# Forgetting attention: decay added by VectorE with the row maximum; second top-16 step over 112 sums instead of 256

## The reference

```python
# forgetting attention, 8 heads of 128
s = jnp.einsum('bqhd,bkhd->bhqk', qb, k) * scale
s = s + (F[q] - F[k])            # F = cumsum(log sigmoid(forget logit))
p = jax.nn.softmax(jnp.where(q_pos >= k_pos, s, NEG_INF))
# PEER routing, 8 heads, 128 + 128 keys
v1, i1 = lax.top_k(s1, 16);  v2, i2 = lax.top_k(s2, 16)
cand = v1[..., :, None] + v2[..., None, :]          # 16 x 16 = 256 sums
sc, sel = lax.top_k(cand.reshape(..., 256), 16)
expert = i1[sel // 16] * 128 + i2[sel % 16];  gate = softmax(sc)
```

## Time and profile before

| | us |
|---|---|
| median of 3 runs (4210.09 to 4221.3) | 4219.01 |
| the profiled execution | 4219.77 |
| its span, first to last instruction | 4218.0 |
| PE busy (matmul) | 3439.9 |
| DVE busy | 2838.2 |
| POOL busy | 1438.0 |
| ACT busy | 381.5 |
| granted TensorE clock, mean | 0.90 |
| DMA, mean over the span | 335 GB/s |

### The profile page before, as it was taken

How to read it: one execution, slowest core, us unless ns; L and a number is a source line. 1 busy time by engine, 2 the same in 40 slices (tenths; PEclk the granted TensorE clock), 3 DMA queues, 4 the chain that set the end, 5 groups by cost and what they waited for, 6 DMA issues and landing times.

```text
span 4218.0 us, 39029 instructions
## 1 busy us (share of the span) xinstructions
PE 3439.9 (82%) x14249; PEld 2539.4 (60%) x14249; DVE 2838.2 (67%) x3456; ACT 381.5 (9%) x954; POOL 1438.0 (34%) x1094
## 2 busy tenths in 40 slices
PE   7899999999999989999988789999939999930000
PEld 5466678888845546567766567777727777720000
DVE  5354442237777875775677888887885555579998
ACT  0311110000211111010000011001000000010000
POOL 0000000000025443442343442324352665577764
PEclk9999999999999998989999899999969999965555
DMA  8577555567359998999999996889989999989997
GB/s 326 209 273 291 207 198 207 200 235 277 147 235 397 375 375 353 389 374 381 415 409 411 412 374 270 316 333 383 417 334 377 419 409 409 413 312 408 410 396 319
DMA packets 251315, 1412.71 MB, mean 335 GB/s; under 512 B 35313, under 2 KB 83457, under 8 KB 86145
## 3 DMA queue, kind: packets, MB, share of 16 engines
q0 software_dynamic: 124704, 841.18, 49.5%
q1 hardware_dynamic: 68832, 501.25, 30.4%
q10 hardware_dynamic: 57632, 68.41, 4.6%
HBM read 1359.60 MB, written 51.16 MB: 334 GB/s over the span
## 4 chain that ended last, share of the span: by engine, by line
PE 42%; DMA 22%; DVE 20%; POOL 7%; issue 4%; DVEq 2%; ACT 1%; PEld 0%; ACTq 0%; PEldq 0%; SPq 0%; POOLq 0%
PE pq L434 42%; DMA first<-peer_v,experts 10%; DMA first<-peer_u,experts 9%; DVE pq L1727 5%; POOL first L1885 4%; DVE late L1727 3%; DVE first L1717 3%; DMA ring<-wstream 3%; POOL got L1903 2%; DVE ring L1266 1%; DVE late L1264 1%; DVE arena L1500 1%; DVE arena L1507 1%; POOL ring L1885 1%; DVE arena L1501 1%
## 5 line engine op out<-in xcount | busy, mean ns | idle before, releaser
L434 PE MATMUL pq<-h_last,ring 128*128 128x288 f32 (+2 forms) x6688 | 1670.7, 412 | 52.0 <-DVEq L1469 34.5
L434 PEld LDWEIGHTS pq<-h_last,ring 128*128 128x128 f32 (+2 forms) x6688 | 1272.9, 191 | 440.7 <-DVEq L1469 38.1
L1885 POOL DMA_INDIRECT first<-peer_u,experts x256 | 394.3, 1540 | 1734.8 <-DVEq L1562 1213.1
L1885 POOL DMA_INDIRECT first<-peer_v,experts x464 | 640.1, 1380 | 872.4 <-DVEq L1728 788.6
L1727 DVE SCALAR_TENSOR_TENSOR late<-first,wts,late 128x2048 f32<-128x2048 f32 x254 | 597.3, 2351 | 200.7 <-DMA first<-peer_v,experts 189.1
L1717 DVE CUSTOM_DVE_ANT_0 first<-first,late 128x2048 f32<-128x2048 f32 x256 | 582.4, 2291 | 213.1 <-DMA first<-peer_u,experts 204.8
L434 PE MATMUL pq<-first,ring 128*128 128x256 f32 (+2 forms) x3104 | 686.8, 383 | 13.1 <-DMA ring<-wstream 6.6
L434 PEld LDWEIGHTS pq<-first,ring 128*128 128x128 f32 (+2 forms) x3104 | 577.7, 187 | 116.1 <-issue 10.5
L1727 DVE SCALAR_TENSOR_TENSOR pq<-first,wts,pq 128x2048 f32<-128x2048 f32 x142 | 334.4, 2355 | 113.2 <-DMA first<-peer_v,experts 103.9
L1903 POOL DMA_INDIRECT got<-dots_dram,at_dot x288 | 322.8, 1121 | 105.6 <-issue 105.0
L434 PE MATMUL pq<-arena,ring 128*128 128x256 f32 (+2 forms) x1216 | 298.4, 406 | 43.0 <-issue 30.4
(11 more groups left out here) (197 smaller groups left out, 2061.7 us busy)
## 6 DMA issues: line engine op xcount, KB each, us to landing
ring<-wstream SPq DMA_DIRECT2D x478, 1024.0 KB
dots_dram<-wts ACTq DMA_DIRECT2D x8, 2304.0 KB, 8.4
dots_dram<-stage ACTq DMA_DIRECT2D x128, 144.0 KB
first<-peer_v,experts POOLq DMA_INDIRECT x464
got<-dots_dram,at_dot POOLq DMA_INDIRECT x288
first<-peer_u,experts POOLq DMA_INDIRECT x256
out<-arena ACTq DMA_DIRECT2D x6, 512.0 KB, 7.5
o_last<-x_t ACTq DMA_DIRECT2D x5, 576.0 KB, 17.0
```

What stands on the lines that cost most here:

```text
L434: return nc.tensor.matmul(out, lhsT, rhs, start=start, stop=stop)
L1885: g.indirect_dma_start(out=slots[slot], out_offset=None, in_=peer_u if kind == "u" else peer_v, in_offset=bass.IndirectOffsetOnAxis(ap=exp ...
```

## The change

The decay leaves the matmuls. `frow` keeps only -F; one DRAM tensor `forget` holds it, and `load_forget` (one DMA on ACT's queue) broadcasts one head's row to all 128 partitions: 256 elements in group 0, 672 in group 1. DVE waits for it ahead of `row_max`, which adds it to the scores in PSUM and takes the maximum in one instruction, `tensor_tensor_reduce`. F[q] is left out: it is the same for a whole row, so the softmax does not see it. The stores and loads of the rows of ones go.

The second `top16` looks at 112 sums: those of the 4 best of the first list with all 16 of the second, and those of the 12 others with the 4 best of the second. A pair (a, b) of ranks counted from 0 is beaten by (a+1)(b+1) - 1 others, so no other pair can be among the 16 best. The position has to be decoded in another way, and the picking of the two halves is no longer in pairs but one after the other. Some renamings are left out below.

```diff
-        aug_q = [area("misc", WG[1], 2), area("latT", WG[1], 2, NH * PAST)]
-        aug_k = [area("misc", NKEY, 2, WG[1]), area("latT", NKEY, 2, NH * PAST + WG[1])]
+        forget = [area("misc", NKEY), area("latT", NKEY, P, NH * PAST)]
...
+        NF = 4 * TOPK + 4 * (TOPK - 4)
...
+                self.cand, self.cand_rest = self.pairs[:, :, 0:NF], pairs_rest[:, :, 0:NF]
+                self.cand_wide = self.pairs[:, :, 0:4 * TOPK].rearrange("p t (a b) -> p t a b", a=4)
+                self.cand_deep = self.pairs[:, :, 4 * TOPK:NF].rearrange("p t (a b) -> p t a b", b=4)
...
             def scores_fox(g, h):
-                if g == 0:
-                    pe.wait_ge(aug_in[0], 32 * (h + 1))
-                else:
-                    pe.wait_ge(aug_in[h % 2], 32 * (h // 2 + 1) + (32 * NH if h % 2 == 0 else 0))
...
-                    for c0, c1, keys_of, at in parts:
-                        mm(ps[:, c0:c1], qn[:, q], keys_of, True, False)
-                        last = mm(ps[:, c0:c1], aq[:, q], ak[:, at:at + c1 - c0], False, True)
+                    for c0, c1, keys_of in parts:
+                        last = mm(ps[:, c0:c1], qn[:, q], keys_of)
...
-            act.dma_start(aug_q_dram[:, 1, :], aug_ones[:, 0:T]).then_inc(aug_st, 16)
-            act.dma_start(aug_k_dram[:, 0, :], aug_ones).then_inc(aug_st, 16)
...
-                act.dma_start(aug_q_dram[:, 0, CG[g]:CG[g + 1]], frow[:, 0, 0:w]).then_inc(aug_st, 16)
                 kw_ = w + (PAST if g else 0)
-                act.dma_start(aug_k_dram[:, 1, CG[g]:CG[g] + kw_], frow[:, 1, 0:kw_]).then_inc(aug_st, 16)
+                act.dma_start(forget_dram[:, CG[g]:CG[g] + kw_], frow[:, 0:kw_]).then_inc(forget_st, 16)
...
-            def load_aug(g, i):
+            def load_forget(g, i):
                 b = i % 2 if g else 0
-                act.dma_start(aug_q[b][:, 0:WG[g]], aug_q_dram[i, :, CG[g]:CG[g + 1]]).then_inc(aug_in[b], 16)
                 kw_ = NKEY if g else WG[0]
-                act.dma_start(aug_k[b][:, 0:kw_], aug_k_dram[i, :, 0:kw_]).then_inc(aug_in[b], 16)
+                act.dma_start(forget[b][:, 0:kw_], forget_dram[i:i + 1, 0:kw_].to_broadcast([P, kw_])).then_inc(forget_in[b], 16)
...
             def evict_fox(g, i):
                 if i > 0:
                     act.wait_ge(kt_ps, NH * g + i)
+                    act.wait_ge(mx_ok, head(g, i, True))
                     if g == 0:
                         act.wait_ge(kA_st, 16 * i)
-                        load_aug(0, i)
+                        load_forget(0, i)
...
-                    v.reduce_max(stat[0:m, 2, t:t + 1], pb[b][0:m, c:c + SC_W[g][i]], AX.X)
+                    d = pb[b][0:m, c:c + w]
+                    if less is None:
+                        v.reduce_max(stat[0:m, 2, t:t + 1], d, AX.X)
+                    else:
+                        k0 = 0 if t < QT else TP
+                        v.tensor_tensor_reduce(out=d, in0=d, in1=less[0:m, k0:k0 + w], scale=1.0, scalar=-3.0e38,
+                                               op0=ALU.add, op1=ALU.max, accum_out=stat[0:m, 2, t:t + 1])
...
-                    row_max(g, head(g, i, True), cn["mask_fox"], 1.0)
+                    if g == 0:
+                        dve.wait_ge(forget_in[0], 16 * (i + 1))
+                    else:
+                        dve.wait_ge(forget_in[i % 2], 16 * (i // 2 + 1) + (16 * NH if i % 2 == 0 else 0))
+                    row_max(g, head(g, i, True), cn["mask_fox"], 1.0, forget[i % 2 if g else 0])
...
-                    va = r.top_v[:, :, 0, :].rearrange("p t (k o) -> p t k o", o=1).to_broadcast(full)
-                    vb = r.top_v[:, :, 1, :].rearrange("p t (o k) -> p t o k", o=1).to_broadcast(full)
-                    v.tensor_tensor(r.hots[0], va, vb, ALU.add)
+                    for dst, a0, a1, nb in ((r.cand_wide, 0, 4, TOPK), (r.cand_deep, 4, TOPK, 4)):
+                        part = [P, nt, a1 - a0, nb]
+                        va = r.top_v[:, :, 0, a0:a1].rearrange("p t (k o) -> p t k o", o=1).to_broadcast(part)
+                        vb = r.top_v[:, :, 1, 0:nb].rearrange("p t (o k) -> p t o k", o=1).to_broadcast(part)
+                        v.tensor_tensor(dst, va, vb, ALU.add)
...
                     v.tensor_scalar(r.sel_a, r.sel, 4, None, ALU.logical_shift_right)
-                    v.tensor_scalar(r.sel_b, r.sel, 15, None, ALU.bitwise_and)
-                    dve.drain()
-                    v.tensor_copy(r.sel_f[:, 0], r.sel_a)
-                    v.tensor_copy(r.sel_f[:, 1], r.sel_b)
+                    v.tensor_scalar(r.sel_b, r.sel, 2, None, ALU.logical_shift_right)
+                    dve.drain()
+                    v.scalar_tensor_tensor(r.sel_f[:, 0], r.sel_b, -12.0, r.sel_a, ALU.add, ALU.max)
                     dve.drain()
...
+                    v.tensor_scalar(r.ex_f, r.sel_f[:, 0], 4.0, 48.0, ALU.mult, ALU.add)
+                    chosen(0)
+                    dve.drain()
+                    v.scalar_tensor_tensor(r.ex_f, r.sel_f[:, 0], 16.0, r.ex_f, ALU.mult, ALU.min)
+                    dve.drain()
+                    v.tensor_tensor(r.sel_f[:, 1], r.sel, r.ex_f, ALU.subtract)
+                    numbered(0)
+                    dve.drain()
+                    v.reduce_sum(r.sel_f[:, 0], r.hots[0], AX.X)
+                    chosen(1)
+                    dve.drain()
+                    numbered(1)
+                    dve.drain()
+                    v.reduce_sum(r.sel_f[:, 1], r.hots[1], AX.X)
```

More of the change, by code:

```diff
@@ L164, in build @@
     dots_dram = nc.dram_tensor("dots_dram", (NK * NK, TD), F32).ap()
-    aug_k_dram = nc.dram_tensor("aug_k", (NH, 2, NKEY), F32).ap()
+    forget_dram = nc.dram_tensor("forget", (NH, NKEY), F32).ap()
     with ExitStack() as ctx:
@@ L207, in build @@
         F_W = WG[1] + PAST
-        frow = area("probT", 2 * F_W, NH).rearrange("p (r t) -> p r t", r=2)
+        frow = area("probT", F_W, NH)
         merged = [arena[:, 0:KC * w].rearrange("p (k t) -> p k t", k=KC) for w in WG]
@@ L244, in __init__ @@
                 self.s_rest = route(nl * NK, "p (t s n) -> p t s n", t=nt, s=2)
-                self.cand = route(nt * NC, "p (t n) -> p t n", t=nt)
+                self.pairs = route(nt * NC, "p (t n) -> p t n", t=nt)
                 self.top_v = route(nl * TOPK, "p (t s k) -> p t s k", t=nt, s=2)
@@ L254, in __init__ @@
                 self.sel_b = route(nt * TOPK, "p (t k) -> p t k", U32, t=nt)
-                self.cand_rest = self.s_rest.rearrange("p t s n -> p t (s n)")
-                self.hots = [x.rearrange("p t (k j) -> p t k j", k=TOPK) for x in (self.cand, self.cand_rest)]
+                pairs_rest = self.s_rest.rearrange("p t s n -> p t (s n)")
+                self.hots = [x.rearrange("p t (k j) -> p t k j", k=TOPK) for x in (self.pairs, pairs_rest)]
+                self.cand, self.cand_rest = self.pairs[:, :, 0:NF], pairs_rest[:, :, 0:NF]
+                self.cand_wide = self.pairs[:, :, 0:4 * TOPK].rearrange("p t (a b) -> p t a b", a=4)
+                self.cand_deep = self.pairs[:, :, 4 * TOPK:NF].rearrange("p t (a b) -> p t a b", b=4)
         routing = [Routing(len(GT[g]), WG[g]) for g in range(2)]
@@ L323, in build @@
         kA_st, kA_in = sem("kA_st"), [sem(f"kA_in{b}") for b in range(2)]
-        aug_in = [sem(f"aug_in{b}") for b in range(2)]
+        forget_in = [sem(f"forget_in{b}") for b in range(2)]
         kt_ps, kt_ok, kt_out = sem("kt_ps"), sem("kt_ok"), sem("kt_out")
@@ L596, in scores_fox @@
                     if t == QT:
[L597 removed]
+                        parts = [(0, TS, kn[:, 2 * P:2 * P + TS]), (TS, TS + PAST, kf_past[:, h, :])]
                     else:
[L599 to L603 removed]
+                        parts = [(0, CG[1], kA[:, h % 2, :])] if g == 1 else []
+                        parts.append((own, (t + 1) * P, kn[:, 0:(t + 1) * P - own]))
+                    for c0, c1, keys_of in parts:
+                        last = mm(ps[:, c0:c1], qn[:, q], keys_of)
                 last.then_inc(s_ok, 1)
@@ L1390, in latents, with row_max @@
                 dve.wait_ge(cum_ps, g + 1)
-                v.tensor_copy(frow[:, 0, 0:2 * P], pb[5][0:NH, 0:2 * P])
-                fw_ = w
+                v.tensor_scalar(frow[:, 0:2 * P], pb[5][0:NH, 0:2 * P], -1.0, None, ALU.mult)
                 if g == 1:
-                    v.tensor_copy(frow[:, 0, 2 * P:w], pb[6][0:NH, PAST:PAST + TS])
-                    v.tensor_copy(frow[:, 0, w:w + PAST], pb[6][0:NH, 0:PAST])
-                    fw_ = w + PAST
-                dve.drain()
-                v.tensor_scalar(frow[:, 1, 0:fw_], frow[:, 0, 0:fw_], -1.0, None, ALU.mult)
+                    v.tensor_scalar(frow[:, 2 * P:w], pb[6][0:NH, PAST:PAST + TS], -1.0, None, ALU.mult)
+                    v.tensor_scalar(frow[:, w:w + PAST], pb[6][0:NH, 0:PAST], -1.0, None, ALU.mult)
                 dve.drain().then_inc(frow_ok, 1)
-            def row_max(g, n, mask, scale):
```

(5 more changed lines are left out.)

27 lines of the change are left out of this document (11 added, 16 removed).

## The result

| | before | after |
|---|---|---|
| median, us (5 runs each) | 4213.29 (4207.39 to 4221.3) | 4180.79 (4173.15 to 4183.42) |
| ratio | | 0.9917 [0.990, 0.9934] |
| the profiled execution, us | 4219.77 | 4178.11 |
| PE busy, us | 3439.9 | 3382.4 |
| DVE busy, us | 2838.2 | 2814.8 |

The change takes 32.5 us by the medians (35 by the ratio, 28 to 42 by its interval), where the sum said 21.3.

The account below looks back on a forecast made before the run. No engine was taken to bound the whole; each edit was priced in its own stretch. The terms -4.4 - 0.4 - 14.6 - 1.9 = -21.3 us gave 4198 us for the median, range 4181 to 4215.

Parts of the forecast that it names:

- Part 3: Routing of group 1: DVE saves 1.83 us in each of 8 heads, -14.6 us (bounds -8 and -18).
- more rows fall beside PE's laps and fewer into the stall: Between group 1's routing and the sort: a loss from DVE being earlier, taken as even with the sort's steps hiding.
- Part 4: FoX heads of group 1: faster scores less the cost of loads and accumulator reads, -1.9 us (-12 to +7).
- Half goes, -3.4: Group 1's FoX head 0: half of the 6.73 us of twelve score matmuls goes, -3.4 us.
- In heads 1 to 3 I take 1.5: Group 1's FoX heads 1 to 3: 1.5 us gained of at most 3 x 3.48, gather waits taking the rest.
- From head 4 on not at all: Group 1's FoX from head 4 on: DVE does not wait for PE's scores, being late behind its gathers; no gain.
- PE was the bound of group 1's FoX: Rival: every head's wait shrinks and the clock rises; group 1's FoX -12 to -20, total about -35, 4184 us; chance 0.10.
- Part 1: FoX heads of group 0: five heads on the path save 1.03 less 0.16 us each, -4.4 us (0 to -5.2).
- Part 2: Routing of group 0: -3.2 us at the gather, but PE gains only a few tenths; -0.4 us (0 to -3.2).
- small steps eat the routing gain: Rival: group 1's decoding costs 1.3 us a head more; Part 3 is -4, total about -11, 4208 us; chance 0.12.
- The broadcasts collide: Rival: all 6.3 us of group 1's decay-row loads delay gathers; Part 4 becomes +4, total -15.4; chance 0.14.
- The decay row: Rival: in group 0 the row lands late and DVE waits; at 20 us, total +28, 4247 us; chance 0.03.

Follow-up runs that it names:

- e_pe_late: The changed kernel with an extra, overwritten 2-row matmul ahead of each FoX score matmul in heads 4 to 7 of group 1; 4186.78 us, 0.9948 of before.
- e_pe_g0: The changed kernel with an extra, overwritten 2-row matmul ahead of each FoX score matmul in group 0 alone; 4190.69 us, 0.9956 of before.
- e_route_g1: The changed kernel with group 0's routing in its old form (256 sums, old decoding), group 1's in the new one; 4186.07 us, 0.9935 of before.
- e_dma_g1: The changed kernel with each decay-row broadcast of group 1 done twice, the second into a place nothing reads; 4186.82 us, 0.9929 of before.
- v_sort: v_split with the sort's last ten steps behind every gathered row instead of every second one; 4157.26 us, 0.9858 of before.
- v_split: The changed kernel with DVE's 7 gathered rows per routed head taken as 3 in the middle of routing and 4 after it; 4149.33 us, 0.9863 of before.

## Why the prediction was right and wrong

**Part 3, routing of group 1: right in its sum, by two errors that cancel.** DVE's own work in the routed head, from its first MAX8 to the end of the expert numbers, fell from 22.16 to 20.30 us, 1.86, where 1.83 was said. The periods of heads 1 to 7 fell by 2.5 each (309.6 as the mean of two kernels, 292.2 of nine), since waits for gathers shrank too, which was not foreseen. But from the last routed head to the sort's end it now takes 5.0 more (291.2 and 296.2). That is where the prediction took "more rows fall beside PE's laps and fewer into the stall" and "the sort's wide steps hide" as even. With head 0, which has no interval of its own and is given DVE's 1.9: -17.3 - 1.9 + 5.0 = -14.2 for the -14.6 of the sum. That they agree is luck.

**Part 4, FoX of group 1: wrong, and it is the step that failed.** It said -1.9; the means are 317.0 (seven kernels with nothing put back) against 331.3 (three with PE's full time), -14.3. Three of its readings failed.
- "Half goes, -3.4": 6.73 became 2.16. The unit price assumed that PE's time is in proportion to the instructions. The clock of the earlier trace rows, 0.86, was at hand and was used only for a rival's price; it was low because of the matmuls that the change removes, so removing them paid twice, in the scores and in the projection behind (17.41 before, 15.69 after). From the score group of head 1 to that of head 2 PE took 28.1 us and now takes 21.6, 6.5 less, nearly twice the 3.4.
- "In heads 1 to 3 I take 1.5": head 0 to head 3 took 86.6 us before and 82.2 after.
- "From head 4 on not at all": heads 4 to 7 took 85.0 and 78.8. The prediction asked whether DVE waits for PE's scores, found no such wait, and took PE for idle cover. Its own row says 83.97 busy of 85. e_pe_late puts PE's time back in just these heads, and 8 us of FoX come back. PE's time shows as DVE's waits for gathered rows: 19.6 us of them with the old scores, 11.4 with the new ones, 19.0 with PE's time put back. By what way a full PE lengthens those waits was not found.

The rival "PE was the bound of group 1's FoX" had the mechanism and the price (-12 to -20 for part 4), with a chance of 0.10; what it left out is why the clock was low. Its sum of 4184 is the nearest to the result. What now limits that stretch is DVE with its gathered rows, at a DMA share of 0.99: PE waits 9.51 us for DVE's division in a head that had no idle time before.

**Part 1, FoX of group 0: right within what the runs can tell.** -4.9 by the means of three and ten kernels for -4.4, -3.3 without e_pe_g0, whose time, 10 to 13 us above after, stays unexplained. By heads it went another way than said: 1.23 us for every head, and some 2 us more of waiting for a block at every second one. The cost of the instruction is right as well (0.14 for the accumulator where 0.08 was taken, streaming as priced), and the load was early: 128 KB landed in 3.1 us, where 9.2 was the bound.

**Part 2, routing of group 0: too small.** -0.4 was said, with 3.2 as the other end; about 4 us is what the means show at the last routed head, and 5 to 8 in the time of e_route_g1. The prediction named the gather, 3.2 earlier, and then followed PE, for which it found cover. The cover is not there: PE's transposes behind DVE come 4.27 us earlier, 2 more than FoX of group 0 had gained by then. And the gathers start with DVE's last routed head whatever PE does; that their rows are what the stretch up to the sort has to get through is argued, not shown. Of the 4 us, some 2 lie in the eight routed heads (112.4 from the first to the last, against 114.2 to 114.9); the rest lies between merge and routing, and its cause was not found.

**The sum.** -4.9 - 4.3 - 14.3 - 14.2 = -37.7 from the intervals; the ratio gives -35, 28 to 42. The rival "small steps eat the routing gain" is out (7.16 us of decoding for 7.18). "The broadcasts collide" is neither shown nor excluded: e_dma_g1 prices all of them at 0 to 9, and part 4 gains in spite of them. The decay row was never late. The result lies 0.2 us beyond the low end of the range. The range stood on a median of before of 4219.01 us from three executions; with five it is 4213.29. As a difference the low end was -38, close to the four lower bounds together (-5.2 - 3.2 - 18 - 12 = -38.4), and -32.5 lies inside it. So the 5.7 us of the starting value put the result outside. What is wrong in the sum is its size, 21.3 for some 35, and 12.4 of that is part 4, whose -14.3 is past its own bound of -12.

**The path.** "PE stands 66.66 us until the sort, so what DVE saves ahead of it moves the sort, last laps and tail" gave the right answer for the change: the sort comes 42.3 us earlier and what follows takes as long as before. v_sort shows that the reason was incomplete: taking the sort alone forward past its rows gains nothing. With v_split beside it, in which the rows come earlier too, it points to the row stream as what has to be earlier.

## What to carry to other kernels

Before an engine is called cover because nobody waits for it, read its busy time in that stretch: 83.97 of 85 us can be a bound, and an engine beside it that waits for other transfers may show those waits instead. A full engine is not proof either: PE is busy 333.00 of 333 us while group 1 is routed and stands for 66.66 us soon after. Putting the time back in those heads alone, as e_pe_late does, decides. Read the granted clock of a group before pricing its instructions by count: matmuls over a few rows cost more than their number, and what follows them pays as well. Where a consumer frees no slot for 20 us, give it some of its rows in the middle; that was worth 28 us here, nearly as much as the whole change, with nothing removed.

## What had not been expected of the hardware

- Matmuls over 2 rows lower the granted clock though PE is busy without a gap: 0.80 and 0.78 in score groups with them, 1.00 in the same groups without them or with the same matmuls over 128 rows; 24 instructions take 6.99 us and 3.96.
- The Trainium skill's rule that PE falls to the lower clock after idling is the other case, and here the trace agrees ("TensorE: Matmul & The Clock Gate", section "HAM oscillation — how this bites in real kernels"): behind a pause of 9.51 us the granted clock is 0.51 and 24 score instructions take 8.12 us, and 4.45 where PE had come without a pause.
- `tensor_tensor_reduce` that adds, writes PSUM back and takes the maximum streams at nearly the pace of the reduce alone: 0.73 us for 512 elements against 0.68, plus 0.14 for the accumulator.
